# Block sums of the hidden activations stored to DRAM, their slices loaded by the second product, and VectorE instead of ScalarE and GpSimd taking one partial product out of PSUM

## The reference

```python
def sq_relu_ffn(h, w1, w2):
    return jnp.square(jax.nn.relu(h @ w1)) @ w2
...
        f_p = sq_relu_ffn(modulated_norm(x_p, norm2_g[i], sh2_p, sc2_p), ffn_w1[i], ffn_w2[i])
        x_p = x_p + gt2_p[:, None, :] * f_p
```

## Time and profile before

| | |
|---|---|
| median of 3 runs | 2893.41 us |
| the profiled execution | 2895.44 us |
| its span from first to last instruction | 2893.8 us |
| TensorE busy | 2676.5 us (92%) |
| VectorE / GpSimd / ScalarE busy | 1812.8 / 1183.7 / 1146.9 us |
| mean granted TensorE clock | 0.981 |
| front, hidden, output stage of layer 0 | about 954 to 997, 997 to 1340, 1340 to 1743 us |
| hidden and output stage of layer 1 | about 2141 to 2484, 2484 to 2887 us |

### The profile page before, as it was taken

How to read it: one execution, slowest core, us unless ns; L and a number is a source line. 1 busy time by engine, 2 the same in 40 slices (tenths; PEclk the granted TensorE clock), 3 DMA queues, 4 the chain that set the end, 5 groups by cost and what they waited for, 6 DMA issues and landing times.

```text
span 2893.8 us, 45017 instructions
## 1 busy us (share of the span) xinstructions
PE 2676.5 (92%) x16628; PEld 2360.4 (82%) x16628; DVE 1812.8 (63%) x2502; ACT 1146.9 (40%) x2330; POOL 1183.7 (41%) x1022
## 2 busy tenths in 40 slices
PE   6989999899999899999998988999979999998987
PEld 4877878799988799998776766888879999776766
DVE  4577787655566734437888885224673344878886
ACT  3355555345453322224343433223332322444342
POOL 1122102166543322224788871000332222588886
PEclk9999999899999999999999998999999999999999
DMA  6244434322244222233322355125323222432325
GB/s 238 70 163 142 158 109 149 120 67 67 72 147 148 88 93 92 108 108 131 101 85 77 109 146 150 44 66 179 125 79 115 93 92 99 139 102 76 110 77 98
DMA packets 161007, 320.59 MB, mean 111 GB/s; under 512 B 15604, under 2 KB 105876, under 8 KB 157528
## 3 DMA queue, kind: packets, MB, share of 16 engines
q1 hardware_dynamic: 157352, 305.69, 31.6%
q0 software_dynamic: 3504, 12.91, 2.3%
HBM read 249.34 MB, written 69.21 MB: 110 GB/s over the span
## 4 chain that ended last, share of the span: by engine, by line
PE 43%; DVE 15%; issue 7%; POOL 3%; ACT 1%; DMA 1%; SPq 0%; DVEq 0%; POOLq 0%; ACTq 0%
PE psum L110 14%; PE psum L112 14%; PE psum L111 14%; DVE half_acc L3227 3%; DVE half_s0r_lo L3199 1%; DVE half_s1q_lo L3194 1%; DVE half_s_lo L3203 1%; DVE half_s2r_lo L3199 1%; DVE half_s1r_lo L3199 1%; DVE half_s0q_lo L3194 1%; PE psum L3575 0%; DVE half_w1q_lo L3183 0%; DMA gate_w_raw<-in_cm_w_in 0%; DVE half_w2q_lo L3183 0%; DVE half_w0q_lo L3183 0%
## 5 line engine op out<-in xcount | busy, mean ns | idle before, releaser
L2938 POOL TENSOR_TENSOR half_acc<-half_acc,half_tmp 128x512 f32<-128x512 f32 x176 | 309.2, 1810 | 129.7 <-ACT half_tmp L2674 88.8
L2674 ACT ACTIVATE half_tmp<-psum 128x512 f32<-128x512 f32 x176 | 104.4, 593 | 295.5 <-PE psum L112 293.4
L3227 DVE TENSOR_TENSOR half_acc<-half_acc,psum 128x512 f32<-128x512 f32 x240 | 161.4, 678 | 85.0 <-PE psum L112 82.8
L3103 DVE TENSOR_TENSOR half_piece<-psum,half_snap_p 128x576 f32<-128x576 f32 (+1 forms) x34 | 24.5, 721 | 297.9 <-PE psum L112 297.9
L2569 ACT ACTIVATE half_snap_u<-psum 128x288 f32<-128x288 f32 x128 | 52.6, 411 | 282.6 <-PE psum L112 282.6
L110 PE MATMUL psum<-half_h_hi,half_w0q_hi 128*128 128x288 f32 x512 | 154.0, 301 | 6.9 <-DVE half_h_lo L3068 4.5
L111 PE MATMUL psum<-half_h_lo,half_w0q_hi 128*128 128x288 f32 x512 | 152.2, 297 | 0.0
L110 PE MATMUL psum<-half_h_hi,half_w1q_hi 128*128 128x288 f32 x512 | 151.8, 297 | 0.1
L112 PE MATMUL psum<-half_h_hi,half_w0q_lo 128*128 128x288 f32 x512 | 151.7, 296 | 0.0
L111 PE MATMUL psum<-half_h_lo,half_w1q_hi 128*128 128x288 f32 x512 | 151.0, 295 | 0.0
L112 PE MATMUL psum<-half_h_hi,half_w1q_lo 128*128 128x288 f32 x512 | 150.5, 294 | 0.0
(11 more groups left out here) (750 smaller groups left out, 9485.0 us busy)
## 6 DMA issues: line engine op xcount, KB each, us to landing
scratch_hid<-half_piece SPq DMA_DIRECT2D x64, 576.0 KB, 3.1
patt_mod_w<-in_ada_w_ffn SPq DMA_DIRECT2D x32, 768.0 KB
half_w0q_raw<-in_w SPq DMA_DIRECT2D x24, 1024.0 KB, 5.8
half_w1q_raw<-in_w SPq DMA_DIRECT2D x24, 1024.0 KB, 5.8
patt_mod_w<-in_ada_w_att SPq DMA_DIRECT2D x16, 1024.0 KB, 5.0
half_s0q_raw<-scratch_hid SPq DMA_DIRECT2D x22, 512.0 KB, 3.7
half_s1q_raw<-scratch_hid SPq DMA_DIRECT2D x22, 512.0 KB, 3.7
half_s2q_raw<-scratch_hid SPq DMA_DIRECT2D x20, 512.0 KB
```

Of the source, the lines that this page charges most:

```text
L2674: act.activation(out, psum[:, o_bank_of(product, j), :], ACT.Copy).then_inc(a.c.taken, 1)
L2938: pool.tensor_tensor(part, part, a.tmp[(3 * n + m) % 4][:], ALU.add).then_inc(a.c.added, 1 if i % SLABS else 3)
L3103: dve.tensor_tensor(a.piece[i.par][f_][:, cols, side, :], psum[:, b:b + len(grps), 0:GN], snap[:, cols, :], ALU.add).then_inc(a.c.hid_read, 1)
L3227: dve.tensor_tensor(part, part, of, ALU.add).then_inc(a.c.read, 1)
```

## The change

1. The block sums of the hidden rows are made once, by VectorE, in the hidden steps (`block_sums`), instead of by GpSimd on every loaded slice. They are stored to new DRAM scratch (`hid_sums`, `hid_8`) by four more DMAs per pair on SyncE (`store_sums`), and loaded by one more DMA per step and per slab. `s_sums` and `s8_sum` on GpSimd are gone.
2. The squares and block sums of pair i-1 (`finish_rows`) are now the first thing that VectorE does in pair i.
3. In the output steps the snapshot after P1 is taken by VectorE, which adds it to the accumulator itself (`read` of the new C11_FIRST): five reads per step on VectorE in place of four, two snapshots on ScalarE and two adds on GpSimd in place of three. The order around them is new on VectorE, ScalarE and SyncE.
4. In the front, GpSimd's `h_sums` and `h_lo` go to VectorE, and group 1 has the same order of products as group 0.

```diff
-H_ORDER1 = (P1, P2, P5, P6, P7, P4, P3)
-N_READ = 4 * PAIRS + 2
+N_READ = 5 * PAIRS + 2
-C22, C11, C12, C21 = range(4)
+C11_FIRST, C22, C11, C12, C21 = range(5)
...
             def store_piece(a, i, f):
-                sp.wait_ge(a.c.sq_ready, i.count(2, 2 - f))
+                if f == 1:
+                    sp.wait_ge(a.c.sq_ready, i.count(2, 1))
+                else:
+                    sp.wait_ge(a.c.sum_ready, i.count(N_SUM, 1))
...
+            def store_sums(a, i):
+                sp.wait_ge(a.c.sum_ready, i.count(N_SUM, N_SUM))
+                for place, s in enumerate((S1, S2, S4)):
+                    sp.dma_start(hid_sums[i.index(1, 0)][:, :, place, :], a.sums[s][:]).then_inc(a.c.sums_stored, 16)
+                sp.dma_start(hid_8[i.index(1, 0)], a.sum8[:]).then_inc(a.c.sums_stored, 16)
+
+            def store_pair(a, i):
+                store_piece(a, i, 1)
+                store_piece(a, i, 0)
+                store_sums(a, i)
...
                     for i in (Pair(a, 1, m), Pair(a, 2, m)):
                         sp.wait_ge(a.c.hid_ready, i.count(UNITS))
                         load_w1(a, i, 1)
-                        store_piece(a, i, 1)
-                        store_piece(a, i, 0)
+                        store_pair(a, i)
...
+            def block_sums(a, i):
+                dve.wait_ge(a.c.sq_ready, i.count(2, 2))
+                dve.wait_ge(a.c.sums_stored, i.count(64, 1))
...
+                dve.tensor_tensor(x21, x21, x11, ALU.subtract).then_inc(a.c.sum_ready, 1)
+                dve.wait_ge(a.c.sum_ready, i.count(N_SUM, 1))
+                dve.tensor_tensor(s2, x21, x22, ALU.add).then_inc(a.c.sum_ready, 1)
+                dve.wait_ge(a.c.sum_ready, i.count(N_SUM, 2))
+                dve.tensor_tensor(s1, s2, x11, ALU.add).then_inc(a.c.sum_ready, 1)
+                dve.tensor_tensor(s4, x12, s2, ALU.subtract).then_inc(a.c.sum_ready, 1)
+                dve.tensor_tensor(a.sum8[:], flat[0][:, SEQ:], flat[1][:, SEQ:], ALU.add).then_inc(a.c.sum_ready, 1)
+
+            def finish_rows(a, i):
+                square(a, i, 1)
+                square(a, i, 0)
+                block_sums(a, i)
+
+            def hidden_step(a, i, before):
                 both = (0, 1)
+                finish_rows(a, before)
...
                 read_hidden(a, i, C11, both)
                 w1_lo_q(a, i, 1)
                 read_hidden(a, i, C22, both)
                 w1_lo_r(a, i, 1)
-                square(a, i, 1)
                 read_hidden(a, i, C12, both)
-                square(a, i, 0)
...
                 if product == P6:
-                    pe.wait_ge(a.c.taken, 3 * n + 1)
+                    pe.wait_ge(a.c.read, read_done(n, C11_FIRST))
...
+                    read(a, n, C11_FIRST)
+                    if not last and j == (2 if fresh else 1):
+                        w2_lo_q(a, i + 1, 0)
+                    if not last and not fresh and j == 2:
+                        w2_sums(a, i + 1, 1)
+                    if not last and j == 3:
+                        w2_lo_q(a, i + 1, 1)
+                    if fresh and j == 0:
+                        square(a, Pair(a, FFS - 1), 1)
+                        square(a, Pair(a, FFS - 1), 0)
                     read(a, n, C22)
-                    if not last and j >= 2:
-                        w2_lo_q(a, i + 1, j - 2)
+                    if fresh and j == 0:
+                        block_sums(a, Pair(a, FFS - 1))
+                    if more:
+                        s_lo_q(a, n + 1)
                     read(a, n, C11)
                     if more:
-                        s_lo_q(a, n + 1)
+                        s_lo_r(a, n + 1)
...
                     read(a, n, C12)
-                    if more:
-                        s_lo_r(a, n + 1)
+                    if not last and j == 0:
+                        w2_sums(a, i + 1, 0)
                     read(a, n, C21)
```

More of the change, by code:

```diff
@@ L2045, in __init__ @@
                       for par, kbs in enumerate(((192, 196.5), (201, 154)))]
+        self.sums = {s: sb(f"sum{s}", kb, [P, PAIRS, P]) for s, kb in ((S1, 144), (S2, 176), (S4, 184))}
+        self.sum8 = sb("sum8", 217.25, [P, P])
         self.snap_p1 = sb("snap_p1", wb + 59, [P, 2, GN])
@@ L2264, in steps_of, with snapshot @@
         return range(STEPS * a.layer, STEPS * (a.layer + 1))
+    def snapshot(a, n, m):
+        if n % STEPS == 0:
+            return a.acc[5][:, 512:]
+        return a.tmp[(2 * n + m) % 4][:]
     def acc_part(a, j, c):
-        side, half = ((1, 1), (0, 0), (0, 1), (1, 0))[c]
+        side, half = ((0, 0), (1, 1), (0, 0), (0, 1), (1, 0))[c]
         return a.acc[2 * j + side][:, half * 512:half * 512 + 512]
@@ L2385, in hidden_steps @@
                 load_s8(a, slab)
+                load_w2(a, slab + 1, 0)
+                load_w2(a, slab + 1, 1)
+                store_pair(a, i)
             def output_steps(a):
@@ L2669, in take @@
                 else:
-                    k = 3 * n + m
-                    if i % SLABS:
-                        act.wait_ge(a.c.added, 3 * n - (3, 1, 2)[m])
-                    out = a.tmp[k % 4][:]
+                    if i % SLABS or j == 3:
+                        act.wait_ge(a.c.added, 2 * n + m - 3)
+                    if n % STEPS == 1:
+                        act.wait_ge(a.c.sums_stored, 64 * FFS * (a.layer + 1) + 1)
+                        act.wait_ge(a.c.piece_stored[1][0], pieces_done(a, 1, SLABS))
+                    out = snapshot(a, n, m)
                 act.activation(out, psum[:, o_bank_of(product, j), :], ACT.Copy).then_inc(a.c.taken, 1)
@@ L2963, in project_steps @@
                     w1_sums(a, Pair(a, 2, m), 1)
-                for n in range(2):
-                    s_sums(a, STEPS * a.layer + n)
             def output_steps(a, extra=lambda j, place: None):
@@ L3120, in hidden_step @@
                     read_hidden(a, i, C22, both)
+                    w2_lo_r(a, slab, 0)
                     w2_sums(a, slab, 1)
-                    w2_lo_r(a, slab, 0)
                     s_lo_q(a, n)
@@ L3144, in first_hidden @@
                 norm(a, SAMPLE)
+                h_lo(a, 0, HT4)
+                read_hidden(a, i, C22, (0,))
+                h_lo(a, 0, HB22)
                 read_hidden(a, i, C11, (0,))
[L3146 to L3148 removed]
                 h_sum(a, HT1, 1)
[L3150 removed]
+                h_lo(a, 1, HB11)
                 h_sum(a, HT2, 1)
+                h_lo(a, 1, HT1)
+                read_hidden(a, i, C12, (0,))
                 h_sum(a, HT4, 1)
[L3153 to L3156 removed]
+                h_lo(a, 1, HT2)
+                h_lo(a, 1, HB21)
+                h_lo(a, 1, HT3)
+                h_lo(a, 1, HT4)
+                read_hidden(a, i, C22, (1,))
+                h_lo(a, 1, HB22)
                 read_hidden(a, i, C11, (1,))
[L3158 removed]
                 w1_lo_q(a, i, 1)
+                w1_lo_r(a, i, 1)
                 read_hidden(a, i, C12, (1,))
[L3161 to L3163 removed]
             def w2_sums(a, i, e):
@@ L3235, in read_8 @@
                     else:
-                        dve.wait_ge(a.c.read, (i - 1) * N_READ + 4 * PAIRS + half + 1)
+                        dve.wait_ge(a.c.read, (i - 1) * N_READ + 5 * PAIRS + half + 1)
                         dve.tensor_tensor(part, part, psum[:, 6 + half, :], ALU.add).then_inc(a.c.read, 1)
@@ L3349, in edge @@
             def edge(j, place):
-                if j == 2 and place == 1:
-                    split_w(0)
-                    split_w(1)
-                if j == 3:
+                if j == 2 and place < 2:
+                    split_w(place)
+                if j == 3 and place < 2:
                     gate_norm(place)
-                    if place == 1:
-                        split_w(2)
+                if j == 3 and place == 1:
+                    split_w(2)
+                if j == 3 and place == 2:
+                    gate_hT(0)
+                    split_w(3)
+                    gate_hT(1)
             project_steps(first, 2)
             output_steps(first, edge)
-            split_w(3)
-            split_w(4)
-            gate_hT(0)
-            split_w(5)
-            gate_hT(1)
-            for n in range(6, 2 * KT):
+            for n in range(4, 2 * KT):
                 split_w(n)
@@ L3449, in hidden @@
                 if product == P3:
-                    pe.wait_ge(a.c.hid_read, hid_reads(i, 3 * grp + 2 if i.first else 2))
+                    pe.wait_ge(a.c.hid_read, i.count(3, (1, 4)[grp], 3) if i.first else hid_reads(i, 2))
                 for k in range(GK):
@@ L3524, in project_steps @@
                 i = Pair(a, 0)
-                for grp, order in enumerate((H_ORDER, H_ORDER1)):
-                    for product_ in order:
+                for grp in range(2):
+                    for product_ in H_ORDER:
                         hidden(a, i, product_, grp)
```

264 lines of the change are left out of this document (112 added, 152 removed).

## The result

The changed kernel takes 2966.27 us (median of 4 runs, 2964.41 to 2972.97), the kernel before 2894.24 beside it: ratio 1.0253, 95% interval [1.0235, 1.0272]. It is slower by 72 us; the forecast was 49, its range held the time.

| part | before, us | after, us | measured | forecast |
|---|---|---|---|---|
| pairs 1 to 14 | 317.70 + 316.57 | 383.36 + 381.44 | +130.5 | +130 |
| pair 15 | 25.39 + 25.39 | 28.45 + 30.42 | +8.1 | 0 |
| slab 0 | 50.56 + 50.37 | 54.23 + 53.58 | +6.9 | 0 |
| slabs 1 to 6, twelve | 49.81 each | 46.07 each | -44.9 | -53 |
| slab 7 | 53.96 + 50.03 | 51.47 + 48.05 | -4.5 | -4 |

The account below looks back on a forecast made before the run. TensorE was taken as the bound, without waits in the hidden steps, with waits in output steps and front. From 2895.4 us, +130 - 53 - 4 - 24 gave 2944, or 2942 at the median, 1.7% slower; range 2886 to 3000.

Parts of the forecast that it names:

- The load: Hidden steps: weight load queued behind sum stores lands 6.3 us later, 4.7 us a pair over 28 pairs, +130 us.
- the allowance: Hidden steps: 0.3 us taken for what the weight load loses behind the stores, from between 0 and 1.9.
- the upper bound: Hidden steps: weights 7.9 us later with the full 1.9 lost behind the stores, 28 x 6.3 = +175 us.
- 22.40 + delay - 1.64: Hidden steps: pair length as today's 22.40 us plus the weights' delay less the slack; 4.7 us longer was forecast.
- The slack of 1.64 us: Hidden steps, kernel before: VectorE's read of C22 ends at +17.56, P3 needs it and starts at +19.20.
- the first rival's second half: Hidden steps: stalls lower TensorE's clock for half of the P3s, 45 us more, 2987; whole rival's chance 0.17.
- The last pair ... I count 0: Pair 15: loads equally late, but VectorE already the one waited for at the stage's edge; 0 us.
- Slab 0, "I count 0": Output steps, first slab: it also has the last pair's squares and sums; counted as 0 us.
- the 5 a layer: Edge from hidden to output steps: allowance of 5 us a layer either way around a count of 0.
- The output steps: Six full slabs a layer, each 4.4 us shorter as GpSimd's work shrinks: -53 us (4 to 76).
- a smaller toll, 0.5 us: Output steps: GpSimd's work lengthens a VectorE instruction with two SBUF inputs by 0.5 us, less than full exclusion.
- The front: Front: norm ends some 4.7 us earlier with `h_sums` and `h_lo` on VectorE; 12 us a layer, -24 (14 to 34).
- The rival in which the load comes in time: Hidden steps: weights land no more than 1.64 us later, nothing of the 130 appears, 2812 us; chance 0.08.

Follow-up runs that it names:

- experiment 1: The change with SyncE issuing each pair's weight load ahead of the six stores of the pair before: 2815.96 us, ratio to before 0.9737.
- experiment 4: The kernel before with one edit, SyncE issuing a pair's weight load only when P6 of the pair is through: 3025.21 us, ratio 1.0465.
- experiment 2: The change with SyncE's weight load behind the two row stores and ahead of the four stores of block sums: 2841.90 us, ratio 0.9828.
- before, after P5 (5): The kernel before with one edit, SyncE's weight load waiting for P5 of its pair: 2916.45 us, ratio 1.0088.
- third dose (3): The change with SyncE's weight load behind the two row stores and two of the four sum stores: 2963.57 us, ratio 1.0248.
- experiment 6: The change with output-step weight sums moved from VectorE to GpSimd and the first unit's block split moved to step 2: 2954.40 us, ratio 1.0221.
- experiment 9: Experiment 1 with P1's output-step snapshot back on ScalarE and its add on GpSimd, block sums in DRAM kept: 2774.21 us, ratio 0.9597.
- experiment 8: Experiment 7 with the split of the first unit's sums moved from step 2 to the end of step 3: 2782.61 us, ratio 0.9619.
- experiment 7: The change with both edits, weight load ahead of the stores and output-step weight sums on GpSimd: 2806.25 us, ratio 0.9709.
- experiment 10: Experiment 8 with GpSimd's front weight sums of pair 1 placed after its second h_t3: 2779.14 us, ratio 0.9610.

## Why the prediction was right, and where it was not

**The load (+130, measured +130.5).** The mechanism is shown from both sides: taking the delay out of the change ends both waits (experiment 1), putting only the delay into the kernel before makes them (4). That the number came out to 0.5 us is luck, since four sizes were off and cancelled. SyncE's distance from sum store to sum store is 0.74 us, not the 0.59 taken from the earlier trace rows, and the load goes out at +9.96 in the mean, 0.9 later than forecast. It then lands in 5.3 us in the mean, not in 5.95 + 0.3 (the earlier trace rows and the allowance): behind the sum stores it was not held up, against 5.0 in experiment 4, which has none. The Trainium skill's rule that descriptors are taken in ring order (DMA: Bandwidth & Descriptors, "Queues, rings and completion order") therefore did not bring the upper bound; in the pair shown of experiment 2, where the load stands between stores, it lost 1.4. Together the delay was 6.2 in place of 6.3, which makes 127 us. To these come 10 us of clock, which the sum did not have, and 7 go, because the first pair of each layer's loop took 26.5 and 25.4 us already in the kernel before, where the sum had 22.40. All doses side by side, each value the mean of the 28 pairs:

| kernel | first sum, after P1 | 22.40 + delay - 1.64 | mean pair | pairs with slow P3 |
|---|---|---|---|---|
| load first (1) | +5.4 | 22.40, in time | 22.41 | 0 |
| small dose (2) | +11.5 | 23.2 | 23.3 | 1 |
| before, after P5 (5) | +11.8 | 23.5 | 23.5 | 0 |
| third dose (3) | +14.3 | 26.0 | 27.3 | 26 |
| before, after P6 (4) | +15.0 | 26.7 | 27.3 | 13 |
| the change | +15.3 | 26.9 | 27.3 | 8 |

The slack of 1.64 us and a slope of 1 hold at every dose, and pair by pair: each pair of the five late kernels has the formula's length within 0.15 us, or 1.35 to 1.56 more where its P3 ran slow. Of the change's 383.36 us in layer 0, 313.69 are the matmuls at full clock, 52.0 are waits, and 17.7 are longer matmuls; a part of these stands within a wait that they shorten and costs nothing, a slow P4 above all. What the clock adds to the time is the slow P3s: 8 of 28, 12 us in all and about a quarter of the 45 in the first rival's second half. The 10 us above are these, less what the other pairs lie below the formula.

**"The last pair ... I count 0" (measured +8.1).** This step failed. VectorE was held to be what the edge waits for; it was the loads of the output weights behind the same stores (experiment 1: 22.91 us, less than before). VectorE, far from being late, sits idle for 9 us until the first of them has landed, and its sums, ScalarE's splits and then the snapshot that P4 needs come after it. In pair 15 of layer 0 of the changed kernel, VectorE's first weight sum and TensorE's wait:

```profile
1385.97 0.69 DVE L3179 TENSOR_TENSOR half_w0r_raw<-half_w0q_raw 128x512 f32<-128x512 f32 x1 [8.96 <-DMA half_w0q_raw<-in_w]
PE psum L110 <- ACT half_snap_u L2601: 4.4, 1, 4.4
```

**Slab 0, "I count 0" (+6.9).** Here VectorE is late: squares, block sums and the fifth read are new in its queue. With the last pair, it is 15 us in all, over the 5 a layer that the forecast allowed for both. The wait list of the slab in the changed kernel:

```profile
PE psum L110 <- DVE half_acc L3233: 4.3, 3, 2.8
PE psum L110 <- DVE half_s1q_lo L3200: 1.1, 1, 1.1
```

Less on VectorE brings it back (50.5 in experiment 6, 49.0 in 9); what the squares and block sums cost alone was not tried.

**The output steps (-53, measured -44.9).** The mechanism is right, two sizes were small: the matmuls of a slab take 43.8 and not 43.5 (experiment 8), and the two waits before P6 cost 2.3 us (1.5 of idle time, the rest in the slower matmuls behind them) and not 1.9. GpSimd's adds and VectorE's weight sums and weight splits are shorter, as forecast; the splits of the slices are not (`s_lo_q` 1.78 us in the mean against 1.63). Groups of the changed kernel, 1590 to 1682 us (line, operation, busy us, mean ns):

```profile
L2931 POOL TENSOR_TENSOR half_acc<-half_acc,half_tmp 128x512 f32<-128x512 f32 x16 | 20.9, 1307 | 71.2 <-ACT half_tmp L2708 71.2
...
L3195 DVE TENSOR_TENSOR half_w1r_lo<-half_w1r_raw,half_w1r_hi 128x1536 fp32r<-128x1536 f32 x1 | 1.7, 1746 | 0.0
```

and of the kernel before, 1590 to 1690 us:

```profile
L3188 DVE TENSOR_TENSOR half_w1r_lo<-half_w1r_raw,half_w1r_hi 128x1536 fp32r<-128x1536 f32 x1 | 2.2, 2248 | 0.0
```

The adds fell from 1836 ns to 1307. VectorE is busy 40.54 us of a slab with four more reads, 42.21 without them: 4.4 us came back for 2.7 spent. But the sum never asked what the two halves are worth singly; experiment 9 does, and there they have opposite signs. The prediction's reading of the earlier trace rows, "a smaller toll, 0.5 us", does not hold as a rule: in experiment 7 the toll is about what the other engine has left to run, 0.57 us on VectorE's split (2.85 - 2.28) and 2.06 on GpSimd's sum (3.35 - 1.29).

**The front (-24, measured -15.4).** The wait for `half_h` fell from 4.5 to 0.9, as forecast. The waits for `half_h_lo` did not fall (4.7 us against 4.3), and the clock did not come back (0.90 against 0.92). Mis-sized were the splits: moved to VectorE they were taken at 1.3 us each, and several took 2.1 to 2.25 beside GpSimd's weight sums, which had stayed. That this is what holds up TensorE is not shown (experiment 10).

**The other side.** The rival in which the load comes in time was priced at 2812 us. Experiment 1 made it so and took 2816. The nearness is in part luck: output steps and front gave back 15 us less than the forecast had, slab 0 cost 6, and against these stand 7 us of the loop's first pairs and 5 of pair 15.

## What to carry to other kernels

An in-order queue that issues loads must not have an issue in it that waits for late work ahead of a load that is ready to go: here one swap of two lines on SyncE was worth 150 us. When a change bundles several edits, price each alone, above all those that lengthen the queue of an engine that another waits for: a slab went from 49.81 to 43.9 us with the sums in DRAM and the new order, and the fifth read took 2.2 of that back. A wait on the path is not the end of its price; look at the stretch behind it for the clock, and whether another wait stands behind that stretch, which can take up the loss.
